# Four overflow pairs under one branch, and the second tile's fetched rows added in an earlier stage of a two-block transformer kernel

## What is computed

```python
for l in range(DEPTH):                                  # 2 layers
    ...
    x = layer_norm(ALPHA * x + g1x * yx, ln1_g[l], ln1_b[l])
    ux = x * (1.0 + s2x) + sh2x
    y = hier_moe(tok, w_grp, b_grp, w_rexp, b_rexp, w_gate, w_up, w_down)   # 32 experts
    x = layer_norm(ALPHA * x + g2x * y[:t], ln2_g[l], ln2_b[l])

def run(args):                                          # inside hier_moe, for each expert
    xb, e = args
    h = silu(xb @ w_gate[e]) * (xb @ w_up[e])           # 1024 -> 512
    return h @ w_down[e]                                # 512 -> 1024
```

## Time and profile before

| | |
|---|---|
| median of 3 runs | 2521.93 us (2518.14 to 2523.73) |
| the profiled execution | 2522.74 us, of which the span is 2520.9 us |
| PE busy | 2255.7 us, 89% of the span |
| DVE, ACT, POOL busy | 935.8, 371.7, 133.8 us |
| DMA | 687.01 MB, mean 273 GB/s |

### The profile page before, as it was taken

One profiled execution on the slowest core, in us unless ns is written; L12 is line 12 of the kernel. 1 busy time (PEld: TensorE's weight loads), 2 busy tenths in 40 slices (PEclk: granted clock), 3 DMA queues, 4 the chain that ended last, 5 costly groups with the idle time before them and its releaser, 6 DMA issues. The chain is left out here.

```text
span 2520.9 us, 35294 instructions
## 1 busy us (share of the span) xinstructions
PE 2255.7 (89%) x14014; PEld 1214.8 (48%) x14016; DVE 935.8 (37%) x1642; ACT 371.7 (15%) x633; POOL 133.8 (5%) x202
## 2 busy tenths in 40 slices
PE   6999877998888877997789999997899999989999
PEld 2443744443333323334433333333566777666776
DVE  3865667420000017777653111112443233582001
ACT  1000413111111101005211111110161000110000
POOL 1001010000000011010100000000111010000000
PEclk8999888999999988999889999999899999999999
DMA  9768421999999992791389999997325786434442
GB/s 357 279 253 330 150 70 67 372 422 422 423 423 423 423 395 92 255 362 51 136 350 422 422 422 422 422 422 302 132 73 188 283 304 238 161 100 150 152 156 77
DMA packets 174193, 687.01 MB, mean 273 GB/s; under 512 B 13813, under 2 KB 72181, under 8 KB 111648
## 3 DMA queue, kind: packets, MB, share of 16 engines
q1 hardware_dynamic: 159712, 625.38, 63.7%
q0 software_dynamic: 11392, 48.90, 5.4%
q10 hardware_dynamic: 3008, 11.62, 1.4%
HBM read 670.99 MB, written 13.81 MB: 272 GB/s over the span
## 5 line engine op out<-in xcount | busy, mean ns | idle before, releaser
L1644 PE MATMUL bank<-ring,arena 128*32 128x512 f32 (+1 forms) x3072 | 341.6, 598 | 39.4 <-issue 20.9
L517 PE MATMUL bank<-ring,actT 128*128 128x512 f32 x768 | 338.1, 601 | 7.9 <-issue 3.3
L2954 PE MATMUL bank<-actT,ring 128*128 128x256 f32 x1344 | 293.4, 379 | 0.0
L2954 PEld LDWEIGHTS bank<-actT,ring 128*128 128x128 f32 x1344 | 255.2, 190 | 42.3 <-issue 8.6
L1677 PE MATMUL bank<-arena 128*32 128x512 f32 (+1 forms) x2048 | 226.6, 594 | 21.2 <-ACT arena L1779 21.2
L1845 DVE TENSOR_TENSOR arena<-arena,bank 128x512 f32<-128x512 f32 x32 | 22.0, 687 | 594.8 <-ACT arena L1774 594.8
L517 PEld LDWEIGHTS bank<-ring,actT 128*128 128x128 f32 x768 | 147.2, 193 | 198.1 <-issue 193.2
L1644 PEld LDWEIGHTS bank<-ring,arena 128*32 128x32 f32 x3072 | 99.6, 111 | 275.5 <-issue 274.5
L595 DVE SCALAR_TENSOR_TENSOR arena<-ring,cols,arena 128x2048 f32<-128x2048 f32 x84 | 195.0, 2349 | 53.1 <-DMA ring<-ada_w 51.2
L2966 PE MATMUL bank<-ring,arena 128*128 128x512 f32 x352 | 154.6, 593 | 0.0
L2311 PEld LDWEIGHTS bank<-arena 128*128 128x128 bf16 x2304 | 133.2, 100 | 43.6 <-issue 36.0
(11 more groups left out here) (508 smaller groups left out, 2185.1 us busy)
## 6 DMA issues: line engine op xcount, KB each, us to landing
ring<-moe_w_gate SPq DMA_DIRECT2D x128, 1024.0 KB, 21.0
arena<-moe_w_down SPq DMA_DIRECT2D x128, 1024.0 KB, 21.3
ring<-ada_w SPq DMA_DIRECT2D x72, 1024.0 KB, 7.7
ring<-ffn_w SPq DMA_DIRECT2D x66, 1024.0 KB, 5.4
ring<-moe_w_up SPq DMA_DIRECT2D x64, 1024.0 KB, 23.4
actT<-moe_w_up SPq DMA_DIRECT2D x64, 1024.0 KB, 24.5
arena<-ada_w POOLq DMA_DIRECT2D x24, 1024.0 KB, 9.3
ring<-ab_w_in SPq DMA_DIRECT2D x14, 1024.0 KB, 8.3
```

The lines of the kernel that those rows point to most:

```text
L517: mm = nc.tensor.matmul(self.bank[g % 6][:, :], lhsT(m, k), halves[k // 4][:, k % 4, :], start=(k == 0), stop=(k == KT - 1))
L1644: mm = nc.tensor.matmul(bank[j // 2][Q * q:Q * q + Q, :], A(XS + P * kt + Q * q, Q), weights(j, own, q, k * DE, DE), start=(kt == 0), stop ...
L2954: mm = nc.tensor.matmul(bank[2 - 2 * (j % 2) + which][:, f * SEQ:(f + 1) * SEQ], w[:, k, f * P:(f + 1) * P], self.actT[:, k * T:k * T + SE ...
```

## The change

Behind the main loop, the overflow loop has NOV / 4 turns (2 in layer 0, 1 in layer 1), and each turn holds four overflow pairs under one branch. The number of pairs that run is rounded up to a multiple of 4 (in `overflow_tables`). Pair 14 is taken out of the main loop. The registers that the overflow loop, pair 14 and pair 15 need are all loaded ahead of pair 14 on PE, instead of right before their use; ACT and DVE load theirs ahead as well. In layer 0, tile 1's fetched rows are added by DVE in the experts' stage, behind tile 0's. In `rows_before_c` DVE sums tiles 0 and 1, then modulates both, then sums tiles 2 and 3, then modulates these.

```diff
-                def pair(p, first, own_at, arrived, last=False):
-                    own = [pe.value_load(A(off, Q)[0:1, own_at].bitcast(I32), min_val=0, max_val=1) for off in (OWN, LENT)]
+                def owners(own_at):
+                    return [pe.value_load(A(off, Q)[0:1, own_at].bitcast(I32), min_val=0, max_val=1) for off in (OWN, LENT)]
+
+                def pair(p, first, own, arrived, last=False):
...
-                with pe.Fori(0, LAST) as p:
-                    pair(p, 0, bass.ds(p, 1), lambda m: main_arrived(p, m))
+                with pe.Fori(0, LAST - 1) as p:
+                    pair(p, 0, owners(bass.ds(p, 1)), lambda m: main_arrived(p, m))
                 pe.wait_ge(sc["tables"], 1)
-                there = blocks(pe)
-                with pe.Fori(0, NOV) as q:
-                    with pe.If(there > 2 * q):
-                        pair(q, LAST, bass.ds(q + PAIRS, 1), lambda m: over_arrived(q, m))
-                pair(extra_pairs(pe), LAST, slice(LAST, LAST + 1), lambda m: main_arrived(LAST, m), last=True)
+                there, more = blocks(pe), extra_pairs(pe)
+                own, own_last = [owners(slice(e, e + 1)) for e in (LAST - 1, LAST)]
+                pair(0, LAST - 1, own, lambda m: main_arrived(LAST - 1, m))
+                with pe.Fori(0, NOV // TOGETHER) as turn:
+                    with pe.If(there > turn * (2 * TOGETHER)):
+                        q = turn * TOGETHER
+                        for n in range(TOGETHER):
+                            pair(q, LAST + n, owners(bass.ds(q + (PAIRS + n), 1)), lambda m: over_arrived(q, n, m))
+                pair(more, LAST, own_last, lambda m: main_arrived(LAST, m), last=True)
...
-                    self.add_fetched(dve, link, 0)
+                    for t in range(2):
+                        self.add_fetched(dve, link, t)
...
             add_last(0)
-            for t in range(1, 4):
+            add_last(1)
+            modulate(0)
+            modulate(1)
+            for t in (2, 3):
                 self.add_fetched(dve, link, t)
-                modulate(t - 1)
                 add_last(t)
+            modulate(2)
             modulate(3)
...
-        link(V_.tensor_scalar(A(FIN + 28, n_ob // 2), self.iota[:, 0:n_ob // 2], 2.0, A(CUM + NE - 1, 1), ALU.mult, ALU.is_lt))
+        turns = n_ob // 2 // TOGETHER
+        link(V_.tensor_scalar(A(FIN + 28, turns), self.iota[:, 0:turns], 2.0 * TOGETHER, A(CUM + NE - 1, 1), ALU.mult, ALU.is_lt))
```

More of the change, by code:

```diff
@@ L70 @@
 SUMMED = ((6, 7), (4, 5))
+TOGETHER = 4
 MOE_BUFFERS = (10240, 15104, 12288, 12544, 13568, 14080, 14592, 15240)
@@ L1619, in main_arrived, with over_arrived @@
                         pe.wait_ge(self.spare_in[layer][m - R], p * 16 + 16)
-                def over_arrived(q, m):
-                    pe.wait_ge(self.over_in[layer][m // 2], q * 32 + 32)
+                def over_arrived(q, n, m):
+                    pe.wait_ge(self.over_in[layer][m // 2], q * 32 + (32 * n + 32))
                 def gather(half):
@@ L1737, in _ @@
                 there = blocks(sp)
[L1738 to L1744, removed]
+                with sp.Fori(0, NOV // TOGETHER) as turn:
+                    with sp.If(there > turn * (2 * TOGETHER)):
+                        q = turn * TOGETHER
+                        for i in range(TOGETHER):
+                            a, b = [expert(sp, q * 2 + (2 * i + e)) for e in range(2)]
+                            for m, (src, k, n) in enumerate(self.pair_sources(layer, a, b)):
+                                if m % 2 == 0:
+                                    sp.wait_ge(sc["used"], q * 6 + (6 * (LAST - 1 + i) + m // 2 + 1))
+                                sp.dma_start(view(m, k), src).then_inc(self.over_in[layer][m // 2], 16)
                 more = extra_pairs(sp)
@@ L1802, in _ @@
                 take(1)
-                with act.Fori(0, LAST) as p:
+                with act.Fori(0, LAST - 1) as p:
                     pair(p, 0)
                 act.wait_ge(sc["tables"], 1)
[L1806 to L1810, removed]
+                there, more = blocks(act), extra_pairs(act)
+                pair(0, LAST - 1)
+                with act.Fori(0, NOV // TOGETHER) as turn:
+                    with act.If(there > turn * (2 * TOGETHER)):
+                        q = turn * TOGETHER
+                        for n in range(TOGETHER):
+                            pair(q, LAST + n)
                 if layer == 0:
@@ L1894, in _ @@
                     self.rows_for_c(dve, link)
+                    there, more = blocks(dve), extra_pairs(dve)
                     with dve.Fori(4, LAST) as p:
                         pair(p, 0)
[L1897 to L1901, removed]
+                    with dve.Fori(0, NOV // TOGETHER) as turn:
+                        with dve.If(there > turn * (2 * TOGETHER)):
+                            q = turn * TOGETHER
+                            for n in range(TOGETHER):
+                                pair(q, LAST + n)
                     pair(more, LAST, last=True)
@@ L1923, in _ @@
                     self.context_for_mla(dve, link)
+                    there, more = blocks(dve), extra_pairs(dve)
                     with dve.Fori(2, LAST) as p:
                         pair(p, 0, by_pair(p))
[L1926 to L1930, removed]
+                    with dve.Fori(0, NOV // TOGETHER) as turn:
+                        with dve.If(there > turn * (2 * TOGETHER)):
+                            q = turn * TOGETHER
+                            for n in range(TOGETHER):
+                                pair(q, LAST + n, by_pair(q + (PAIRS + n)))
+                    pair(more, LAST, by_pair(LAST), last=True)
     def combine(self, t, stop, shares=None, to=None):
@@ L2296, in overflow_tables @@
         V_.tensor_copy(A(FIN, 1).bitcast(I32), A(CUM + NE - 1, 1))
-        link(V_.tensor_scalar(A(FIN + 28, n_ob // 2), self.iota[:, 0:n_ob // 2], 2.0, A(CUM + NE - 1, 1), ALU.mult, ALU.is_lt))
-        link(V_.tensor_reduce(A(FIN + 41, 1), A(FIN + 28, n_ob // 2), AX_X, ALU.add))
-        V_.tensor_copy(A(FIN + 40, 1).bitcast(I32), A(FIN + 41, 1))
+        turns = n_ob // 2 // TOGETHER
+        link(V_.tensor_scalar(A(FIN + 28, turns), self.iota[:, 0:turns], 2.0 * TOGETHER, A(CUM + NE - 1, 1), ALU.mult, ALU.is_lt))
+        link(V_.tensor_reduce(A(FIN + 41, 1), A(FIN + 28, turns), AX_X, ALU.add))
+        V_.tensor_scalar(A(FIN + 40, 1).bitcast(I32), A(FIN + 41, 1), float(TOGETHER), None, ALU.mult)
         V_.tensor_scalar(A(FIN + 1, n_ob).bitcast(I32), A(EID, n_ob), float(NE - 1), None, ALU.min)
```

## The result

| kernel | median us (lowest to highest, runs) | time against before, 95% interval |
|---|---|---|
| before, beside it | 2522.05 (2518.14 to 2523.73, 5) | |
| changed | 2507.85 (2507.07 to 2511.5, 5) | 0.9948 [0.9933, 0.9963] |
| changed, a second time | 2508.49 (2499.78 to 2514.39, 6) | 0.9934 [0.9912, 0.9957] |

A forecast was written before the change was run, and what follows sets the result against it. DMA limits the loop; behind it PE idles over empty overflow turns, then waits for DVE's row chain. Stage end 5.6 + chain 9.2 + layer 1 5.0 = 19.8 us off 2521.9: 2502.1 us, range 2498 to 2513.

The forecast's parts named there:

- Branches: PE's branch over the overflow pairs: one 6.0 us fetch per layer; idle before pair 15 4.9 and 3.3 us.
- (a): Layer 0's jump back and second pass each fetch again, three times 6.0 us: 2512.2 us; chance 0.13.
- (b): The fetcher streams through all four pairs' code, 6.0 us a packet, at least three more per layer: 2536 us; chance 0.05.
- Moved loads: Four more register loads before pair 14, 2.6 us: layer 0's 1.9 us delay covered by a weight wait, layer 1 costs 0.2.
- The stage's end in layer 0: Experts' stage, layer 0: DVE becomes last, next stage starts at 941.0 instead of 946.6, 5.6 us gained.
- the worst case of 942.7: Layer 0's stage end: DVE done at 942.7 instead of 940.2 if tile 1's rows take 8.0 us to land.
- Rival (c): Tile 1's rows take 21 us to land beside the projection weights, layer 0's stage loses 9.5 us: 2517.2 us; chance 0.04.
- The rows' chain: DVE's row work before layer 0's projection: two additions of 4.62 us leave the chain, 9.2 us gained.
- rival (d): Only the empty turns bring gain; DVE's order changes nothing, something else holds PE at 974.10: 2511.3 us; chance 0.04.
- Layer 1: Pair 15 in layer 1 starts at 1722.0 instead of 1727.05 us, 5.0 us gained.
- the bound on the good side: Layer 1: 1.9 us more gain if PE's clock does not fall in pair 15's first products.
- Sum: Whole kernel: gains of 5.6, 9.2 and 5.0 us make 19.8 us, giving 2502.1 us.

The follow-up runs named there:

- after_again: The changed kernel run once more, with nothing changed: 2508.5 us, 0.9934 against before.
- rows_only: The kernel before with only VectorE's half (tile 1's fetched rows added in the experts' stage, two sums first): 2517.6 us, 0.9977 against before.
- weights_later: The changed kernel with the next stage's first weights in layer 0 issued only when tile 1's fetched rows are there: 2505.0 us, 0.9924 against before.

## Why the prediction was right, and where it was off

**Branches: right.** One fetch per layer, 6.3 and 6.0 us, with one packet each, and the second pass in 0.22: rivals (a) and (b) are refuted. Idle before pair 15 was to be 4.9 and 3.3 us and is 5.16 and 3.03. From the mark to pair 15 layer 0 gained 8.5 us (7.6 forecast); 1.7 of them are the clock, which fell in pair 14 in the kernel before alone (32 products at 887.46 took 5.34 us, now 3.64). The Trainium skill ("Runtime: NRT & Kernel Launch", section "Instruction fetch mechanics") has a taken branch fetch whenever its target lies outside a two-page window; the second pass of the changed kernel, over four pairs' code, took 221 ns, which does not agree.

**Moved loads: right.** Counted from the mark, pair 14 starts 1.8 us later in layer 0 (1.9 forecast). Its wait for the up weights, 2.31 us, takes in most of that: the weights' products start 0.5 us later than before. In layer 1 pair 14 starts 0.7 us later, but its down products only 0.1 us (29.93 us behind the mark instead of 29.82; 0.2 forecast).

**The stage's end in layer 0: this step failed in size.** It names VectorE and its wait for fetched rows as the new bound, and the trace shows them. But "these times hang on the DMA, not on PE, and do not move" holds for the issue and not for the landing: 8.3 us instead of 5.4. On the time scale of before (1.94 us added), tile 1's rows were there at 938.9 instead of 935.5, VectorE was done at 943.5, behind even the worst case of 942.7, and the stage ended at 944.1. 2.6 us arrived instead of 5.6 (8.5 less the 6.0 that B grew by); against a kernel before without the clock's fall in pair 14 it would be 0.9. Rival (c) had this cause, at 21 us instead of 8.3. PE's side, which was to be ready at 937.6 with the clock kept, did not keep it: pair 15's first 96 products took 12.49 us and not 10.5. PE would have let the stage end at 938.6 (935.15 and 1.94 and 1.5 for the meeting); VectorE's later end hid that.

**The rows' chain.** 9.2 us forecast, 7.5 measured (27.49 to 20.03). The operations left it as counted: with PE's sums at the full clock VectorE's first operation would come 2.0 us behind the stage's start instead of 3.79, which is the missing 1.8. The prediction did not ask what the clock does in a wait that the change itself lengthens (1.5 to 7.0 us). Tile 2 was ready with some 6 us to spare, as forecast; rival (d) is refuted.

**Layer 1.** 5.0 forecast. Pair 15 starts 5.3 us sooner after the mark; the clock then took 0.9 us in its first products and 1.6 in its down products (8.64 us for 7.07), so that 2.8 were left. after_again, where it did not fall, gained 7.4, more than the bound on the good side (6.9).

**Sum.** 2.6 + 7.5 + 2.8 = 12.8 us by the unrounded rows, and 2.1 that came from outside the marks, 1.9 of them ahead of the first: the 14.9 of the spans. Against the sum of 19.8, 3.0 are missing at the meeting, 1.8 in the chain's clock, 2.2 in layer 1's. What came from outside the marks is chance of the clock, and so is the 1.7 us in pair 14 that the traced execution of before had lost: the medians, not these two traces, say that the gain is 14 to 15 us.

## What to carry to other kernels

When an engine's work is brought forward, list what its progress releases: here the next stage's weights, which then go beside the very transfer that the moved work waits for. Work that is hidden under a stage must not end behind it; just after a meeting, partly in VectorE's idle time, the same 4.6 us cost 2.6. A fetch behind a long branch costs nothing where a transfer ends the stage, so the place of a branch matters more than its length; here it is worth moving only in layer 1 (moving the loop ahead of pair 14 was not tried).

## What was not expected of the hardware

An indirect fetch's time to land depends on what is queued beside it: tile 1's took 4.8 to 5.1 us without the weights (rows_only, before, weights_later) and 7.8 to 8.9 in the eight executions read where the weights had been issued ahead of them. The fetch of instructions costs the same 6.0 to 6.3 us over one pair's code and over four. And an idle time of 3 us on PE was followed by the lower clock in one execution (13.38 us for 96 products) and not in another of the same kernel (10.51), so such a term can only be given as a range.
